# Uneven quotas of K, V and U weight tiles per cache quad, and single K and V pages among the Q tiles, in a one-core decoder step

## What is computed

```
z = rmsnorm(x) @ w_in                  # 2048 x 4096: Q, K, V and U (pooling) parts
a = attention(q, k, v)                 # prompt: causal; samples: top 3 of 8 blocks of a paged
                                       # cache of 2048 keys (16 pages of 128 tokens), 8 heads x 128
p = pooling mixer(u)
x = x + concat(a, p) @ w_out           # 2048 x 2048
x = x + (silu(h2 @ w_gate) * (h2 @ w_up)) @ w_down    # width 5632
y = rmsnorm(x)                         # also returned: new K, V rows and pooling history
```

## Time and profile before

| | |
|---|---|
| three timed runs | 1454.62, 1457.61, 1457.80 us, median 1457.61 |
| the profiled execution | 1456.8 us, of which the span of the trace is 1455.0 |
| TensorE (matmul) | 1396.7 us busy, 96% |
| VectorE | 902.3 us, 62% |
| ScalarE | 501.1 us, 34% |
| mean DMA rate | 230 GB/s, 334 MB moved |

### The profile page before, as it was taken

How to read it: one execution, slowest core, us unless ns; L and a number is a source line. 1 busy time by engine, 2 the same in 40 slices (tenths; PEclk the granted TensorE clock), 3 DMA queues, 4 the chain that set the end, 5 groups by cost and what they waited for, 6 DMA issues and landing times.

```text
span 1455.0 us, 34098 instructions
## 1 busy us (share of the span) xinstructions
PE 1396.7 (96%) x13900; PEld 1294.7 (89%) x13900; DVE 902.3 (62%) x1355; ACT 501.1 (34%) x663; POOL 105.7 (7%) x180
## 2 busy tenths in 40 slices
PE   6999999998898999999999999999999999999998
PEld 5987777767555789999999999999999999999997
DVE  4777777767777645787555464646464646455556
ACT  4421221121134234644343433333333333333334
POOL 2127600000000000200000000000000000000002
PEclk9998999999999999999999999999999999999999
DMA  5898999999999865655655555555555555555552
GB/s 189 264 323 294 361 400 403 401 397 393 395 389 369 275 196 179 199 163 176 189 161 170 161 171 161 170 161 169 162 168 164 167 165 165 167 164 168 164 168 95
DMA packets 164616, 334.41 MB, mean 230 GB/s; under 512 B 10271, under 2 KB 54488, under 8 KB 164223
## 3 DMA queue, kind: packets, MB, share of 16 engines
q1 hardware_dynamic: 164519, 333.06, 68.0%
HBM read 328.10 MB, written 5.27 MB: 229 GB/s over the span
## 4 chain that ended last, share of the span: by engine, by line
PE 81%; SPq 9%; DVE 4%; issue 3%; DMA 3%; ACT 1%; DVEq 0%; ACTq 0%
PE banks L1469 24%; PE banks L1470 24%; PE banks L1471 24%; SPq L427 3%; PE banks L1584 3%; SPq L431 3%; PE banks L1566 2%; SPq L449 2%; DMA vpage<-in_cache_v 2%; PE banks L1477 1%; DVE kpage L897 1%; SPq L419 1%; PE banks L1650 1%; DMA vec<-in_pool_scale 1%; PE banks L1600 1%
## 5 line engine op out<-in xcount | busy, mean ns | idle before, releaser
L855 DVE TENSOR_TENSOR w_lo<-w_raw,w_hi 128x1024 fp32r<-128x1024 f32 x360 | 440.9, 1231 | 405.1 <-ACT w_hi L587 404.2
L1469 PE MATMUL banks<-hh,w_hi 128*128 128x288 f32 x2176 | 646.6, 297 | 4.0 <-issue 1.5
L1470 PE MATMUL banks<-hl,w_hi 128*128 128x288 f32 x2176 | 645.1, 296 | 0.0
L1471 PE MATMUL banks<-hh,w_lo 128*128 128x288 f32 x2176 | 642.8, 295 | 0.6 <-issue 0.6
L587 ACT ACTIVATE w_hi<-w_raw 128x1024 fp32r<-128x1024 f32 x360 | 378.7, 1058 | 671.5 <-PE banks L1471 449.6
L1469 PEld LDWEIGHTS banks<-hh,w_hi 128*128 128x128 f32 x2176 | 411.3, 189 | 21.8 <-issue 18.1
L1470 PEld LDWEIGHTS banks<-hl,w_hi 128*128 128x128 f32 x2176 | 411.4, 189 | 1.1 <-issue 1.0
L1471 PEld LDWEIGHTS banks<-hh,w_lo 128*128 128x128 f32 x2176 | 410.3, 189 | 0.6 <-issue 0.6
L1471 PE MATMUL banks<-ah,w_lo 128*128 128x288 f32 x704 | 207.8, 295 | 0.0
L1470 PE MATMUL banks<-al,w_hi 128*128 128x288 f32 x704 | 207.4, 295 | 0.0
L1469 PE MATMUL banks<-ah,w_hi 128*128 128x288 f32 x704 | 206.6, 293 | 0.5 <-DVE al L1288 0.5
(11 more groups left out here) (197 smaller groups left out, 642.5 us busy)
## 6 DMA issues: line engine op xcount, KB each, us to landing
kpage<-in_cache_k SPq DMA_DIRECT2D x128, 512.0 KB, 7.9
vpage<-in_cache_v SPq DMA_DIRECT2D x128, 512.0 KB, 7.1
w_raw<-in_w_gate SPq DMA_DIRECT2D x88, 512.0 KB, 3.6
w_raw<-in_w_up SPq DMA_DIRECT2D x88, 512.0 KB, 3.6
w_raw<-in_w_down SPq DMA_DIRECT2D x88, 512.0 KB, 3.7
w_raw<-in_w_in SPq DMA_DIRECT2D x64, 512.0 KB, 9.3
w_raw<-in_w_out SPq DMA_DIRECT2D x32, 512.0 KB, 4.1
xs<-in_x_prompt SPq DMA_DIRECT2D x2, 1024.0 KB, 7.2
```

The lines of the kernel that those rows point to most:

```text
L855: V.tensor_tensor(w_lo[:, s, :], w_raw[:, s, :], w_hi[:, u, :].bitcast(F32), ALU.subtract).then_inc(lo_ready, 1)
L1469: PE.matmul(o, wh, xh[:, c, :], start=start and i == 0, stop=False)
L1470: PE.matmul(o, wh, xl[:, c, :], start=False, stop=False)
L1471: last = PE.matmul(o, wl, xh[:, c, :], start=False, stop=stop and i == len(chunks) - 1)
```

## The change

```diff
+KVU_COUNT = (1, 1, 1, 3, 2, 1, 1, 2, 2, 2, 2, 2, 2, 2, 3, 3, 2, 2, 3, 2, 2, 2, 2, 1)
+KVU_FIRST = 2
+KVU_AT = [range(KVU_FIRST + sum(KVU_COUNT[:n]), KVU_FIRST + sum(KVU_COUNT[:n + 1])) for n in range(len(KVU_COUNT))]
+BLOCKS_IN = [[k // 4 for k in tiles if k % 4 == 3] for tiles in KVU_AT]
+def split_at_block(n):
+    first = BLOCKS_IN[n][0] if BLOCKS_IN[n] and KVU_AT[n][-1] % 4 != 3 else -1
+    return [k for k in KVU_AT[n] if k // 4 == first], [k for k in KVU_AT[n] if k // 4 != first]
...
-                if k == 6:
+                if k == 4:
                     sp.wait_ge(pages_in, 16)
-                if 6 <= k < 14:
-                    load_k_page((k - 6) // 4, (k - 6) % 4)
-            for k in range(4):
+                if 4 <= k < 12:
+                    load_k_page((k - 4) // 4, (k - 4) % 4)
+                if k == 12:
+                    sp.wait_ge(xT_in, KC)
+                    sp.wait_ge(hist_T, 2)
+                if k >= 12:
+                    load_v_page(0, k - 12)
+            for k in range(KVU_AT[1][-1] + 1):
                 load_kvu(k)
-            load_v(0)
-            load_v(1)
-            load_kvu(4)
-            load_kvu(5)
+                if k < 4:
+                    load_v_page(1, k)
...
-                for k in (2 * n + 6, 2 * n + 7):
-                    if k < KVU_TILES:
+                if n + 2 < len(KVU_AT):
+                    for k in KVU_AT[n + 2]:
                         load_kvu(k)
...   VectorE, quads j = 1 and 2 of batch i
-                take_block(2 * i)
-                lo_kvu(4 * i + 2)
-                turn_k(i, 2)
-                lo_kvu(4 * i + 3)
-                turn_k(i, 3)
-                take_block(2 * i + 1)
-                lo_kvu(4 * i + 4)
+                slot_ends(n)
+                for j in (1, 2):
+                    head, tail = split_at_block(n + j)
+                    lo_kvu(head or tail)
+                    if head:
+                        slot_ends(n + j)
+                        lo_kvu(tail)
+                        turn_k(i, j + 1)
+                    else:
+                        turn_k(i, j + 1)
+                        slot_ends(n + j)
...   TensorE, quads j = 1 to 3 of batch i
                     logits(i, j)
-                    if i == KVU_STEPS - 1 and j == NQUADS - 1:
-                        pe.wait_ge(z_ready, 24)
-                        rows_turned(0)
-                        rows_turned(1)
+                    head, tail = split_at_block(NQUADS * i + j)
+                    last_slot = i == KVU_STEPS - 1 and j == NQUADS - 1
+                    for k in tail if last_slot else head:
+                        kvu_tile(k)
                     if i:
                         values(i - 1, j - 1)
-                    kvu_pair(4 * i + j + 1)
+                    for k in () if last_slot else tail:
+                        kvu_tile(k)
                 if i == KVU_STEPS - 1:
+                    pe.wait_ge(z_ready, 24)
+                    rows_turned(0)
+                    rows_turned(1)
                     rows_turned(2)
                     rows_turned(3)
```

More of the change, by code:

```diff
@@ L438, in load_k, with load_v_page @@
                     load_k_page(n, g)
+            def load_v_page(n, g):
+                sp.dma_start(vpage[:, n % 2, g, :], page(cv, n // NQUADS, 4 * (n % NQUADS) + g)
+                             ).then_inc(v_in[n % 2], 16)
             def load_v(n):
[L442 to L447, removed]
+                sp.wait_ge(v_done, n - 1)
                 for g in range(4):
-                    sp.dma_start(vpage[:, n % 2, g, :], page(cv, n // NQUADS, 4 * (n % NQUADS) + g)
-                                 ).then_inc(v_in[n % 2], 16)
+                    load_v_page(n, g)
             def load_out_pool(ks_):
@@ L626, in _, with hi_kvu @@
                 hi(tile_at(4 + k))
[L628 to L631, removed]
+            def hi_kvu(tiles):
+                for k in tiles:
+                    hi(tile_at(T_KVU + k))
             def save_comb(b):
@@ L886, in x_taken, with lo_kvu @@
                 V.tensor_copy(xT[:, c, :], XB[c % 3][:, 0:T]).then_inc(x_ready, 1)
[L888 to L891, removed]
+            def lo_kvu(tiles):
+                for k in tiles:
+                    lo(tile_at(T_KVU + k))
             def turn_k(i, j, pages_=range(4)):
@@ L923, in _ @@
                     turn_k(0, 0)
-                    lo_kvu(0)
+                    lo_kvu(range(KVU_FIRST))
                 if k % 8 == 7:
@@ L1086, in _, with slot_ends @@
             pad_q(0)
+            def slot_ends(n):
+                for m in BLOCKS_IN[n]:
+                    take_block(m)
             for i in range(KVU_STEPS):
-                lo_kvu(4 * i + 1)
+                n = NQUADS * i
+                lo_kvu(KVU_AT[n])
                 if i:
@@ L1096, in _ @@
                     turn_k(i, 1)
-                take_block(2 * i)
-                lo_kvu(4 * i + 2)
-                turn_k(i, 2)
-                lo_kvu(4 * i + 3)
-                turn_k(i, 3)
-                take_block(2 * i + 1)
-                lo_kvu(4 * i + 4)
-                if i == KVU_STEPS - 1:
-                    rows_out(1)
+                slot_ends(n)
[9 more added lines that the diff above has]
+                        slot_ends(n + j)
+                head, tail = split_at_block(n + 3)
+                lo_kvu(head or tail)
                 scaled_logits(i)
                 pad_q(i + 1)
-                if i == KVU_STEPS - 1:
+                if head:
+                    slot_ends(n + 3)
+                    lo_kvu(tail)
+                if i < KVU_STEPS - 1:
+                    turn_k(i + 1, 0)
+                    if i:
+                        osb_high(i - 1)
+                    if not head:
+                        slot_ends(n + 3)
+                else:
+                    slot_ends(n + 3)
+                    turn_k(i + 1, 0, range(1))
+                    rows_out(1)
+                    turn_k(i + 1, 0, range(1, 2))
                     rows_out(3)
-                turn_k(i + 1, 0)
-                if i:
+                    turn_k(i + 1, 0, range(2, 4))
                     osb_high(i - 1)
@@ L1661, in own_logits @@
                 last.then_inc(so_in, 1)
[L1663 to L1668, removed]
+            for k in range(KVU_FIRST):
+                kvu_tile(k)
             replicate_q()
@@ L1675, in _ @@
                     combine(i - 2)
-                kvu_tile(8 * i + 2)
+                tiles = KVU_AT[NQUADS * i]
+                kvu_tile(tiles[0])
                 if i:
                     joint_max(i - 1)
-                kvu_tile(8 * i + 3)
+                for k in tiles[1:]:
+                    kvu_tile(k)
                 if i:
```

8 lines of the change are left out of this document (5 added, 3 removed).

## The result

The changed kernel takes 1459.31 us (median; 1456.93 to 1462.1) against 1456.28 us (1453.94 to 1457.81) of the kernel before on the same chip. The ratio is 1.0020, with a 95% interval of 1.0014 to 1.0026: 3.0 us slower, where the forecast said 3.7 us faster. The profiled execution has a span of 1457.3 us against 1455.0.

The account below looks back on a forecast made before the run. DMA bytes were taken to bound 155 to 385 us, the engines' chain the first quads. An 8.9 us earlier start less 5.2 for four owed tiles, other parts 0, gave 1457.6 - 3.7 = 1453.9 us, range 1447.5 to 1460.

Parts of the forecast that it names:

- What bounds the kernel: Whole kernel: DMA bytes decide 155 to 385 us, the engines' chain 85 to 148; after 560 us TensorE is full, unchanged.
- Part 1: Q stage: K and V pages of quads 0 and 1 asked for earlier cost 0, bound +1 us; quad 2's K freed.
- Part 2: First four quads: fewer tiles before quad 3's logits bring quad 4's logits 8.9 us earlier, range 7.7 to 10.7.
- The clock part: Quad 4's logits: TensorE keeps full clock because tiles 5 to 7 cover VectorE's work, so they take 2.7 us.
- Part 3: DMA-bound stage: four tiles still owed cost 4 x 1.31 = 5.2 us, leaving a net gain of 3.7 us (2.5 to 5.5).
- P: Moment SyncE asks for K of quad 7, from which the DMA is fed without gap; predicted from 148.1 to 139.2 us.
- Part 4: Batches 3 to 5: more tiles just fit, 0, bound +3 us; SyncE's holds of 5.2 us cost 0, bound +1.7 each.
- B: Rival, late quads: batch 3 needs 58 us instead of 55.2, losing 3 us; 1456.9 us, no change; chance 0.25.
- D: Rival, SyncE's queue: holds idle the DMA 1.7 us at each of five places, 8.5 in all; 1462.4 us; chance 0.11.
- Part 5: Quad 23: tile 47 and the row turns fit into TensorE's 4.5 us wait for V of quad 19: 0, else +4.
- Rival C: Around quad 19's values: tile 47 in the wait removes half clock there and later, about 4 us; 1449.9 us; chance 0.17.
- The sum: Whole kernel: the net gain of 3.7 us moves the median from 1457.6 to 1453.9 us.

Follow-up runs that it names:

- counts_only: Against the kernel after: its tile counts kept, but the K and V pages loaded in the old order; 1458.97 us, ratio 1.0019 to the kernel before.
- owed_late: Against the kernel after: the two tiles taken from quads 5 and 6 come back in quads 17 and 22 instead of 14 and 15; 1458.31 us, ratio 1.0008.
- batch3_nine: Against the kernel after: four tiles still owed, but one goes to quad 10 and batch 3 gets nine tiles instead of ten; 1460.5 us, ratio 1.0025.
- last_quad_none: debt_two with its last tile, 47, in quad 22 and none in quad 23; 1457.53 us, ratio 1.0004.
- debt_two: Against the kernel after: quads 5, 6, 14 and 15 keep two tiles each, so two tiles are owed instead of four; 1455.88 us, ratio 0.9997.

## Why the prediction was wrong, step by step

- **What bounds the kernel** held: 560 us to the end is unchanged, 155 to 385 us is decided by bytes, and what moved the time was how well the DMA was fed.
- **Part 1** (0, bound +1 in the Q stage). The 0 was wrong, and the bound a little short: the new order starts quad 0's logits 1.3 us later, with TensorE waiting for a Q tile between 60 and 85 us in all eleven kernels that have it and in none of the five that don't. That no wait was seen at tiles 7 to 14 before was no ground for the tiles behind them, for which the DMA share is 0.95 instead of 0.70. The emptied queue before K of quad 2 came as said and cost nothing that the other profiles confirm. The part's gain, "K of quad 2 no longer stands behind them", was refuted by counts_only, which reaches quad 2 as soon with V pages ahead of it.
- **Part 2** was mis-sized, and is the largest miss: 8.9 us in the prediction, 5.3 measured (3.6 to 7.0 by the pairs above), below its own range of 7.7 to 10.7. The term that failed is tile 7's landing, put at 3.4 + 12 x 1.31 = 19.1 us after the first K page of quad 2. It took 21.7, and 20.8 at the least in any kernel with the short start. The sum let each request land before the ones behind it moved anything; in the run 1.0 MB of K of quad 4 moved first. The other 0.9 us came between tile 7 and quad 4's logits. The clock part held in this profile: 1.00 at 130 to 140 us and quad 4's logits in 2.76 us. But that was luck: owed_late, which does the same up to there, took 4.08 us for these logits, batch3_nine 4.1, and last_quad_none 4.5 where debt_two, with the same counts there, took 2.8.
- **Part 3** priced a tile owed at 1.31 us by its bytes; owed_late less debt_two gives 1.6 us for two tiles, with an error of 2, so nothing speaks against it. At P 5.3 gained stand against 5.2 owed: nothing of the 3.7 was left. What the step missed is that a tile not asked for saves DMA time only if something else can be asked for instead. At quads 5 and 6 nothing could (share 0.44; 0.55 in owed_late, the same up to there).
- **Part 4** failed at SyncE's queue. Batch 3 took 57.6 us (quad 12 to 16) in place of 55.2. That this is near the 58 of TensorE's sum is chance, as far as the runs show: batch3_nine, with a tile less in the batch, took 57.4. SyncE's hold at tile 28 lasted 7.3 us, more than my 5.2 (the values in it took 3.8 us instead of 1.9, their last matmul starting after a gap of 1.2 us for which the profile names no cause), and the work ahead of it, which I had put at "4 us or more" from the landing times of the earlier trace rows, ran out. The DMA then gave 384 GB/s instead of 401 for 52 us: 0.88 MB, 2.2 us. Rivals B and D met here: the mechanism of D at one place of the five, with about the size of B. My list of places was off by one, too: it lacks tile 33, held for 4.9 us. The hold of 6.5 us at tile 38 took a little (396 GB/s in 284 to 337 us, 399 before); the other three, and the four in owed_late, did fit under the queue.
- **Part 5** held. TensorE's wait for V there is 1.38 us in the kernel after (next row; 4.5 in the earlier trace rows), and last_quad_none, which takes the tile out of quad 23, isn't faster. But V of quad 19 was not ready 3.7 us sooner, as the prediction had it: the values start at 390.45, 5.1 us later than before.
```profile
390.45 1.95 PE L1599 MATMUL banks<-vpage,pT 128*32 128x512 f32 x16 [1.38 <-DMA vpage<-in_cache_v]
```
- **Rival C**: the values there ran in 1.95 us instead of 3.51, so the half clock went at that place, as it said. The later logits did not follow: those of quad 25 took 4.50 us (3.92 in the earlier trace rows), at half clock still. It gained nothing, since the stage was behind by more. The clock fell anew elsewhere, on the values at 226 us; in owed_late, the same up to there, it didn't:
```profile
226.43 3.58 PE L1599 MATMUL banks<-vpage,pT 128*32 128x512 f32 x16 [3.59 <-DMA vpage<-in_cache_v]
...
226.01 1.95 PE L1599 MATMUL banks<-vpage,pT 128*32 128x512 f32 x16 [3.10 <-DMA vpage<-in_cache_v]
```
- **The sum**, by the profiles: -5.3 (Part 2) + 1.3 (Part 1) + 5.2 (Part 3) + 2.2 (Part 4) = +3.4 us, against +3.0 measured (interval 2.0 to 3.8). Against the forecast, Part 2 is off by 3.6 us, Part 4 by 2.2 and Part 1 by 1.3. The fit is better than single profiles warrant, and one thing isn't in it: in the two profiles quad 28's logits start at 439.3 us before and 444.1 after, 4.8 us later, of which 2.5 us are made up by the end of the kernel. Profiles of kernels that are alike there differ by as much (1013.3 us from quad 28 to the end in the kernel after, 1016.3 in counts_only); the cause is open.

What stays open: how the 3.4 us of the two moved tiles divide into the place and the debt. The traces say about 2 for the gap in batch 3, and owed_late, at 1.7 us below the kernel after and 1.6 above debt_two, agrees; its interval overlaps with both. No run changes what is asked for behind tile 7, so that K of quad 4 takes its time is read from the totals and not tested.

## What to carry to other kernels

Where the DMA is full later on, a load that is put off pays only if something else is asked for in its place; look at the share in the stretch where it is taken out. A landing that is waited for is not safe from the requests behind it: count what else will be moving by then. A load that is put somewhere else needs a free slot of its ring at the time of asking, since whatever is behind the waiting request on its queue waits too. Go by how long the hold will be and not by which quads are neighbours: holds of 7 us opened a gap in batch3_nine too, where the two quads of three tiles are apart, and holds of 4.2 us didn't in owed_late, where they are adjacent. Asking later was worse than waiting in all three kernels that tried it. And price a cover by its edge: where Part 4 took 0 for the holds, its bound was the better number.

## What the runs showed of the hardware that was not expected

- A tile asked for before four K pages landed with 1.0 MB of those pages already moved: 12 transfers, 6.29 MB, were down after 21.7 us in which 7.33 MB moved.
- An emptied queue was not slower to bring four pages of 512 KB: 8.6 to 9.5 us in ten kernels, 10.7 in the kernel after, against 9.0, 9.3 and 10.6 in the three kernels with the short start whose queue had not run empty.
- In-order issue on SyncE: a hold of 7.3 us with pages behind it brought a slice of 1.8 us to 204 GB/s; one of 6.5 us brought one to 324, and holds of up to 4.9 us left no mark.
- The half clock at quad 4's logits comes and goes in kernels whose work around it is the same: 2.76 us in the kernel after and in debt_two, 4.08 in owed_late, which does the same as the kernel after up to there. The wait ahead of them was 1.4 and 1.2 us where the clock stayed and 1.9 us where it fell; but quad 2's logits in owed_late kept it after a wait of 2.0 us. One trace of it is no proof that an edit has cured it.
